# A two-block fp32 transformer kernel: dilated attention's steps moved inside the product tiles, the experts' first bias in fp32r, another order of the first loads, the recurrence spread over slots

## The reference, cut to what matters

```
ada = silu(c) @ w_ada + b_ada                       # 6 vectors: shifts, scales, gates
h = rmsnorm(x) * (1 + sc1) + sh1;  proj = h @ w_in + b_in
xr = conv4(xr);  r, i = sigmoid(xr @ w_a), sigmoid(xr @ w_x)   # block diagonal
a = exp(-8 r softplus(-lam));  state[t] = a state[t-1] + sqrt(1 - a*a) (xr i)[t]
y_att = softmax(q k - slope*dist, with a sink) v     # band of 128, 16 heads
x += g1 * rmsnorm(merge(state, y_att) @ w_out)
# experts: logits -> top 4 of 32 -> for each expert
act = swiglu(x_e @ w1[e] + b1[e]);  y += gate * (act @ w2[e] + b2[e])
# second block, layer 1:
qkv = hn @ w_qkv -> 3 groups (dilation 1, 4, 16) x (q, k, v) x 16 heads x 64
q, k = rmsnorm per head;  logits = q k + bias[g, head, distance]
o = softmax over the keys of all three groups together, times v;  h += o @ w_out
```

## Time and profile before

| | us |
|---|---|
| median of 3 executions | 2758.9 (2754.11 to 2763.45) |
| profiled execution, its own time | 2752.79 |
| profiled execution, span | 2751.0 |
| PE busy in the span | 2546.6 (93%) |
| DVE busy | 1377.2 (50%) |
| ACT busy | 1040.5 (38%) |
| matmul clock granted, mean | 0.94 of full |
| memory read | 670 MB, 244 GB/s mean |

### The profile page before, as it was taken

How to read it: one execution, slowest core, us unless ns; L and a number is a source line. 1 busy time by engine, 2 the same in 40 slices (tenths; PEclk the granted TensorE clock), 3 DMA queues, 4 the chain that set the end, 5 groups by cost and what they waited for, 6 DMA issues and landing times.

```text
span 2751.0 us, 36239 instructions
## 1 busy us (share of the span) xinstructions
PE 2546.6 (93%) x13568; PEld 1736.4 (63%) x13569; DVE 1377.2 (50%) x2617; ACT 1040.5 (38%) x1827; POOL 69.9 (3%) x122
## 2 busy tenths in 40 slices
PE   5798969999999999999989999999998999999999
PEld 3566844433343333433348887888886778788788
DVE  4467742111221122112248778776775665554785
ACT  3545531211111111211136555655554665322653
POOL 0000000000000000000000000000001000110000
PEclk8899978999999999999999999999999999656999
DMA  7654347999999999999946555555655445430553
GB/s 269 208 184 153 123 192 290 408 405 410 410 409 409 406 410 401 407 405 411 409 175 199 183 185 168 184 176 177 198 188 157 153 139 170 89 36 4 175 189 126
DMA packets 310572, 673.37 MB, mean 245 GB/s; under 512 B 8421, under 2 KB 235920, under 8 KB 277537
## 3 DMA queue, kind: packets, MB, share of 16 engines
q1 hardware_dynamic: 307280, 663.40, 65.1%
q0 software_dynamic: 3184, 8.53, 2.3%
HBM read 670.25 MB, written 1.12 MB: 244 GB/s over the span
## 4 chain that ended last, share of the span: by engine, by line
PE 78%; DVE 11%; ACT 5%; issue 5%; DMA 1%; POOL 0%; DVEq 0%; ACTq 0%; POOLq 0%
PE PS L349 21%; PE PS L1240 16%; PE PS L350 11%; PE PS L1257 8%; PE PS L1226 4%; PE PS L357 3%; DVE WS L312 3%; PE PS L1749 3%; ACT WS L308 2%; PE PS L1232 2%; PE PS L1770 2%; PE PS L358 2%; PE PS L1757 1%; DVE LIN L1354 1%; DVE AC L1357 1%
## 5 line engine op out<-in xcount | busy, mean ns | idle before, releaser
L349 PE MATMUL PS<-HN,WS 128*128 128x512 f32 x1952 | 702.0, 403 | 20.2 <-DVE WS L312 15.3
L312 DVE TENSOR_TENSOR WS<-RAW,WS 128x1024 fp32r<-128x1024 f32 (+1 forms) x452 | 542.3, 1204 | 224.7 <-ACT WS L308 221.0
L350 PE MATMUL PS<-HN,WS 128*128 128x256 f32 x1952 | 549.5, 282 | 0.0
L308 ACT ACTIVATE WS<-RAW 128x1024 fp32r<-128x1024 f32 (+1 forms) x452 | 465.7, 1035 | 158.5 <-PE PS L358 88.7
L1240 PE MATMUL PS<-W,XG 128*64 128x512 f32 x2048 | 450.4, 598 | 0.0
L349 PEld LDWEIGHTS PS<-HN,WS 128*128 128x128 f32 x1952 | 370.7, 190 | 114.4 <-DVE WS L312 19.0
L1350 DVE TENSOR_SCALAR GLU<-PS 128x512 f32<-128x512 f32 x32 | 22.1, 692 | 729.0 <-PE PS L1240 729.0
L350 PEld LDWEIGHTS PS<-HN,WS 128*128 128x128 f32 x1952 | 373.3, 191 | 0.4
L1240 PEld LDWEIGHTS PS<-W,XG 128*64 128x64 f32 x2048 | 145.0, 138 | 303.9 <-issue 303.9
L1257 PE MATMUL PS<-W,AT 128*64 128x512 f32 x1024 | 226.8, 595 | 22.0 <-ACT AT L1158 22.0
L349 PE MATMUL PS<-MI,WS 128*128 128x512 f32 x704 | 245.4, 394 | 0.0
(11 more groups left out here) (339 smaller groups left out, 2772.2 us busy)
## 6 DMA issues: line engine op xcount, KB each, us to landing
W<-in_moe_w SPq DMA_DIRECT2D x192, 2048.0 KB, 10.7
RAW<-in_ffn_w_in SPq DMA_DIRECT2D x88, 1024.0 KB, 5.2
RAW<-in_attn_w_qkv SPq DMA_DIRECT2D x36, 1024.0 KB, 5.1
RAW<-in_ffn_w_out SPq DMA_DIRECT2D x32, 1024.0 KB, 5.0
RAW<-in_w_ada SPq DMA_DIRECT2D x24, 1024.0 KB, 8.5
RAW<-in_w_in SPq DMA_DIRECT2D x22, 1024.0 KB, 5.2
RAW<-in_ffn_w_out SPq DMA_DIRECT2D x16, 768.0 KB, 4.3
RAW<-in_conv_w_in SPq DMA_DIRECT2D x12, 1024.0 KB, 5.2
```

The source lines that it names most:

```text
L308: act_f(split_tile(0, n), raw_tile(n), ACT.Copy).then_inc(hi_done, 1)
L312: vec.tensor_tensor(split_tile(1, n), raw_tile(n), split_tile(0, n).bitcast(f32), ALU.subtract).then_inc(lo_done, 1)
L349: nc.tensor.matmul(both, hi[:, k, :], x2[:, :, kx, :], start=start, stop=False)
L350: ins = nc.tensor.matmul(half, lo[:, k, :], x2[:, 0, kx, :], start=False, stop=stop)
```

## The change

Six edits. (1) `attention_mixer` is rebuilt: `qk` and `v` become one layer `qkv` of four blocks of 18 tiles. A block holds one turn of four heads: six value tiles, then twelve query and key tiles; QK and VV hold two blocks. The ten steps of turn c stand inside tiles 4 to 10 of block c + 1, one before every sixth chunk, and its outputs are transposed and split behind tiles 11 and 13 there. Steps have one score place, one transpose place and one output place in PSUM; the stage copies (L1847, L1848) and the table ORD with its wait are gone; ACT alone copies the transposed weights. The last turn stands around the first three tiles of `attn_out`. (2) Layers can have three banks; where the number changes between layers, the first tiles wait for all evacuations. (3) In `tok` layers both tiles of a pair are split behind the odd tile. (4) Six `w_ada` pieces are loaded before the first two weight pairs, and the gate weights are loaded before the bias rows are stored. (5) `decay`, the root, the products and the scans are spread over s = 11 to 22. (6) The experts' bias is a high and a low part in fp32r over 128 rows, one matmul per bank; EH becomes 128 x 128.

```diff
+        order = [("ada", j) for j in range(ADA_FIRST - 2)] + [("unit", 0), ("unit", 2)]
+        order += [("ada", j) for j in range(ADA_FIRST - 2, ADA_FIRST)]
+        for n in range(4, len(unit), 2):
...
-            if u.n + SLOTS_W < stop:
+            if not L.tok and u.n + SLOTS_W < stop:
+                make(eng, u.n + SLOTS_W)
+            elif L.tok and u.n % 2:
+                make(eng, u.n + SLOTS_W - 1)
                 make(eng, u.n + SLOTS_W)
...
-                if u.first and L.t0 + u.tile >= 4:
-                    pe.wait_ge(evacuated, L.t0 + u.tile - 3)
+                if u.first and u.tile < L.banks and L.fresh_banks:
+                    pe.wait_ge(evacuated, L.t0)
+                elif u.first and L.t0 + u.tile >= L.banks:
+                    pe.wait_ge(evacuated, L.t0 + u.tile - L.banks + 1)
...
+            pool.wait_ge(sem("ada_mm"), ADA_FIRST - 1)
+            pool.dma_start(BDA[:, :, :], A["bd_a"]).then_inc(sem("bd_loaded"), 16)
+            pool.dma_start(BDX[:, :, :], A["bd_x"]).then_inc(sem("bd_loaded"), 16)
             pool.wait_ge(sem("rows_ready"), N_GROUPS)
...
-                if s in (11, 12):
-                    for c in range(4 * (s - 11), 4 * (s - 10)):
+                if 11 <= s < 15:
+                    for c in range(2 * (s - 11), 2 * (s - 10)):
                         decay(c)
...
+                if s == 15:
                     act.wait_ge(sem("half_tanh"), DC)
                     act_f(T1[:, :, :], T1[:, :, :], ACT.Sqrt).then_inc(sem("rnn_act"), 1)
...
-                if s == 14:
+                if s == 17:
                     dve.wait_ge(sem("rnn_act"), 1)
                     o.link(STT(T1[:, :, :], T3, 1.0, T1[:, :, :], ALU.add, ALU.mult))
...
+                if s == 18:
+                    o.wait()
                     TTN(T2[:, :, :], T2[:, :, :], T1[:, :, :], ALU.mult).then_inc(sem("lru_in"), 1)
-                if s in (15, 16):
+                if 19 <= s < 23:
...
-        sp.dma_start(B1[0:NE, :], A["moe_b1"][0]).then_inc(sem("b1_loaded"), 16)
+        for r in range(4):
+            sp.dma_start(B1[r * NE:(r + 1) * NE, :], A["moe_b1"][0][:, r // 2 * FF:(r // 2 + 1) * FF]).then_inc(sem("b1_loaded"), 16)
...
+            act.wait_ge(sem("b1_loaded"), 64)
+            act_f(B1S[:, :], B1[:, :], ACT.Copy).then_inc(sem("b1_split"), 1)
...
                     for j in range(2):
-                        for g in range(2):
-                            nc.tensor.matmul(bank[j][64 * g:64 * g + 64, :], EH[0:NE, :],
-                                             B1[0:NE, 1024 * g + 512 * j:1024 * g + 512 * (j + 1)], start=True, stop=False)
+                        nc.tensor.matmul(bank[j][:, :], EH[:, :], B1S[:, 512 * j:512 * (j + 1)], start=True, stop=False)
...
+            for half in range(2):
+                h = slice(half * SLOTS, (half + 1) * SLOTS)
+                o.mark(vec.memset(HALVES[h, h], 1.0))
+            for r in range(4):
+                h = slice(r * NE, (r + 1) * NE)
+                o.mark(vec.tensor_copy(PICK[h, :], IDENT[h, h]))
+            dve.wait_ge(sem("b1_split"), 1)
+            for r in (1, 3):
+                low = slice(r * NE, (r + 1) * NE)
+                TTN(B1S[low, :], B1[low, :], B1S[low, :].bitcast(f32), ALU.subtract).then_inc(sem("b1_split"), 1)
...
-                vec.tensor_copy(EH[0:NE, :], IDENT[0:NE, ds(e, 1)].to_broadcast([NE, SLOTS])).then_inc(sem("e_taken"), 1)
+                TS(EH[:, :], HALVES[:, :], PICK[:, ds(e, 1)], None, ALU.mult).then_inc(sem("e_taken"), 1)
...
+        STEP_BEFORE = {(4 + 6 * i // DC, 6 * i % DC): i for i in range(NU + 2)}
+        STEPS_AT = {w: [i for (v, k), i in STEP_BEFORE.items() if v == w + 1] for w in range(3, 10)}
+        LAST_BEFORE = {(1, 0): 0, (1, 3): 1, (2, 0): 2, (2, 3): 3}
+        OUT_AT = {11: 0, 13: 1}
...
             def scores(c, u):
+                pe.wait_ge(sem("q_taken"), 12 * (c + 1))
+                if U:
+                    pe.wait_ge(sem("b_biased"), U)
...
             def turn_keys(c, u):
+                pe.wait_ge(sem("b_exp"), U + 1)
+                if U:
+                    pe.wait_ge(sem("b_ET"), U)
...
             def weigh(c, u):
+                pe.wait_ge(sem("b_ET"), U + 1)
+                pe.wait_ge(evacuated, qkv.t0 + c * TURN_TILES + TURN_V)
+                if U:
+                    pe.wait_ge(sem("b_out"), U)
...
+            def step(c, i):
+                if i < NU:
+                    scores(c, i)
+                if 1 <= i <= NU:
+                    turn_keys(c, i - 1)
+                if i >= 2:
+                    weigh(c, i - 2)
...
+            def last_turn(t):
+                if t == 2:
+                    for i in range(len(LAST_BEFORE), NU + 2):
+                        step(TURNS - 1, i)
+                    for m in (DC - 2, DC - 1):
+                        turn_out(m)
+
+            products(pe, qkv, HN, feed=norm.wait_chunk, after=behind, defer=OPENING, inside=inside)
+            products(pe, ao, OXB, feed=lambda pe, k: pe.wait_ge(sem("ox_lo"), k + 1), defer=(3, DC - 2), between=last_turn,
+                     inside=last_inside)
```

More of the change, by code:

```diff
@@ L327, in run_layer, with dense_bank, products @@
                 behind(u.tile)
-    def products(pe, L, x2, feed=None, after=None, defer=(0, 0)):
+    def dense_bank(L, t):
+        return bank[(L.t0 + t) % 4] if L.banks == 4 else bank[t % L.banks]
+    def products(pe, L, x2, feed=None, after=None, defer=(0, 0), between=None, inside=None):
         fed = set()
@@ L363, in products @@
             for k in range(cut):
+                if inside is not None:
+                    inside(u.tile, k)
                 chunk_of(u, k)
+            if between is not None:
+                between(u.tile)
         for k in range(cut, DC):
@@ new lines, in out_high, with before, behind @@
+            def out_high(m):
+                act.wait_ge(sem("x_T"), m + 1)
+                act_f(OXH[:, m, :], bank[7][:, 0:S], ACT.Copy).then_inc(sem("ox_hi"), 1)
+            def before(s):
+                n = query(s - 1)
+                if n is not None:
+                    square(n, s - 1)
+                n = query(s - 2)
+                if n is not None:
+                    root(n)
+            def behind(s):
+                n = query(s - 3)
+                if n is not None:
+                    take(n)
+                c, w = s // TURN_TILES - 1, s % TURN_TILES
+                if 0 <= c < TURNS - 1:
+                    for i in STEPS_AT.get(w, ()):
+                        step(c, i)
+                    if w in OUT_AT:
+                        out_high(2 * c + OUT_AT[w])
@@ L1685, in work_qk, with work @@
+            def work(t):
                 if t == 0:
@@ L1716, in act, with transposes @@
+                before(t)
+            act.wait_ge(sem("gains_ready"), 6)
+            run_layer(act, qkv, hi_tile, work, behind)
+            for s in range(qkv.T, qkv.T + 3):
+                before(s)
+                behind(s)
+            for i in range(NU + 2):
+                step(TURNS - 1, i)
+            for m in (DC - 2, DC - 1):
+                out_high(m)
             update.act(act)
         def pe(pe):
-            def transposes(t):
-                pe.wait_ge(sem("q_normed"), t + 1)
-                if t >= 2:
-                    pe.wait_ge(sem("q_taken"), t - 1)
+            def transposes(n):
+                pe.wait_ge(sem("q_normed"), n + 1)
+                if n >= 2:
+                    pe.wait_ge(sem("q_taken"), n - 1)
+                if n >= 12:
+                    pe.wait_ge(sem("b_biased"), n // 12 * NU)
@@ new lines, in behind, with inside @@
+            def behind(s):
+                if s == 0:
+                    norm.pe_mean(pe, columns=True)
+                n = query(s - 3)
+                if n is not None:
+                    transposes(n)
+                c, w = s // TURN_TILES - 1, s % TURN_TILES
+                if 0 <= c < TURNS - 1 and w in OUT_AT:
+                    turn_out(2 * c + OUT_AT[w])
+            def inside(t, k):
+                c, at = t // TURN_TILES - 1, (t % TURN_TILES, k)
+                if 0 <= c < TURNS - 1 and at in STEP_BEFORE:
+                    step(c, STEP_BEFORE[at])
@@ L1830, in work_qk, with behind, work @@
+            def behind(s):
+                c, w = s // TURN_TILES - 1, s % TURN_TILES
+                if 0 <= c < TURNS - 1:
+                    for i in STEPS_AT.get(w, ()):
+                        step(c, i)
+                    if w in OUT_AT:
+                        out_low(2 * c + OUT_AT[w])
+            def work(t):
                 if t == 0:
@@ L1901, in dve @@
+                before(t)
+            run_layer(dve, qkv, lo_tile, work, behind)
+            for s in range(qkv.T, qkv.T + 3):
+                before(s)
+            for i in range(NU + 2):
+                step(TURNS - 1, i)
+            for m in (DC - 2, DC - 1):
+                out_low(m)
             update.dve(dve)
```

(3 more changed lines are left out.)

379 lines of the change are left out of this document (168 added, 211 removed).

## The result

The changed kernel takes 2634.97 us (median of 4 runs, 2630.53 to 2636.59), the kernel before 2759.94 (4 runs): ratio 0.9546, 95% interval 0.9528 to 0.9564. Forecast was 2650, range 2614 to 2700. The profiled execution of after has a span of 2634.4 us against 2751.0, so 116.6 us went. The new mean granted clock is 0.968 where it was 0.941.

A forecast was written before the change was run, and what follows sets the result against it. PE bounds nearly everywhere, at half clock in the attention loop, with transfers close beside it in the experts. 5.8 + 13.8 + 10 + 22 + 62 - 4.8 = 108.8 off 2752.8 gives 2644; median offset 6.1: 2650, range 2614 to 2700.

The forecast's parts named there:

- Start, gate weights: Kernel start to mixer tile 14: reordered loads end the transfers' pause, -5.8 us; earlier gate weights remove PE's wait, -13.8 us.
- Recurrence: Mixer tiles from 14 on: spreading decays, root, products and scans over more slots saves 10 us, bounds 4 and 18.
- Experts: Expert loop: cheaper bias, limited by transfers at 30.6 us an expert, plus 14 us of lead: -22 us net, bounds 14 and 43.
- PE waiting for a w1 or w2 landing: Expected sign in the expert loop: PE waits for weight landings, with a period of 30.4 to 30.7 us.
- my own sign of error: Expert loop: the prediction called itself wrong if the period per expert is under 30 us.
- Attention, blocks: The `qkv` blocks: 330 us from first chunk to last, with 31 us of waits and 3.39 us a query tile.
- my sign of error of 0.9: The `qkv` blocks: the prediction called itself wrong if the granted clock there is below 0.9.
- clock rival: Attention steps pull the clock down: to the layer's end, 2830 us, 5%; only in the 21 tiles with steps, 2748, 4%.
- Last turn: Attention's last turn: 51 us, six uncovered steps at the old loop's clock, 5.2 us each; wrong if over 65 us.
- Opening of the next stage: Stage behind attention: PE must wait for all evacuations, so its first tile comes later; 4.8 us charged.
- The rival that ACT and DVE bind: Attention blocks: every step waits for its full chain, 75 us of waits instead of 31, giving 2694 us; 16%.
- The rival that the transfers have room: Expert loop: PE's own 1.4 us per expert count in full, 43 us instead of 22, giving 2629 us; 10%.

The follow-up runs named there:

- experiment 1: The changed kernel with the old order of first loads and the gate weights loaded behind the bias rows again: 2651.6 us, 16.7 more than the changed kernel.
- experiments 5 and 6: Changed kernel with half of each expert's gather, first alone, then also half of w2 for every expert but the first: expert stage 981.9 and 949.2 us.
- experiment 3: The changed kernel with the experts' first bias in fp32 as before, without the set-up of the split bias: 2662.1 us, 27.1 more.
- experiment 8: The changed kernel without projection chunks between the last turn's steps: 63.5 us instead of 50.5 from last query tile to the projection's first evacuation.
- Experiment 10: Also written banks: the changed kernel with the output projection's tiles 3 to 7 in banks the last turn has left: 2626.0 us, ratio 0.9526 to before.
- experiment 5: The changed kernel with each expert's gather for the first 128 tokens alone, loads unchanged: expert stage 981.9 us instead of 986.2.

## Why the prediction was right, step by step

The forecast of 2650 was 15 us too long, 0.6%. About half of that is in the terms: the profiled executions differ by 116.2 us, the terms add up to 108.8. The other half is the 6.1 us that I added because before's median stood above its profiled execution; after's stands 1.6 us below it. By its own steps:

- **Start, gate weights.** 6.3 and 13.5 for 5.8 and 13.8, and the pause of the transfers is gone, as forecast. Undoing both costs 20.1 us at tile 14 (experiment 1).
- **Recurrence.** 7.7 for 10. I counted the new slots' overload but not that the scans, two a slot for four slots, make those tiles slower as well (6.1 us).
- **Experts.** This is the term that was mis-sized: 32.4 for 22. The mechanism, transfers that can't follow and a store that PE eats, was right (experiments 5 and 6). Two sizes were off and worked against each other. The floor is 30.16 us an expert, not 30.6, as I had taken w2's 392 GB/s from a short stretch (and 30.80 less 30.6 is a pause of 0.2 us, not the 0.3 that I summed); and PE saved 1.03, not 1.4, as the bias had been the cover of ACT's copy of XG, which I hadn't looked for. So PE ate 0.4 us an expert, 12 of the 14 us, and never met a landing. "PE waiting for a w1 or w2 landing" was wrong, and so was the period of 30.4 to 30.7: under 30 was my own sign of error. The set-up cost 5.8 for 4, the first expert (gather to w2, 414.75 to 445.7 against 391.59 to 418.75) gained 3.8 for 2.8, and 2.5 us lie behind. Of these, 1.7 are the one slow expert of before (experiment 3) and no part of the mechanism that I forecast; the last 0.8 us I can't place.
- **Attention, blocks.** From first to last chunk 325 us for 330, near by luck in its parts. Waits were 16 for 31. A query tile without steps took 3.24 us for 3.39, some 6 us in all: in the 7.27 us that I had read for two tiles, the wait of 0.51 had cost 0.8 with what stood around it. Against that stand 10 us for six stretches at 0.50 that I had put at nothing, a wait of 2.99 us for the first value tile, and 2 us in steps and outputs. The steps ran mostly at 1.00 in the tiles, as forecast, and the blocks' mean of 0.96 is above my sign of error of 0.9; neither clock rival came true.
- **Last turn.** 50.5 us for 51, by luck in its parts: the last queries took 9.5 for 7.5, the ten steps 34.5 for 39, what follows them 6.5 for 4.5. I forecast the loop's clock for the uncovered six and they had 1.00 for most of the way; experiment 8 shows what that is worth, and on what it hangs.
- **Opening of the next stage.** 6.3 lost for 4.8. Experiment 10 takes exactly that back.

The rival that ACT and DVE bind (2694) was half true at the end of a turn, where the table loads are, and nowhere else. The rival that the transfers have room (2629) gave the nearer number for another reason: they haven't, the store was large enough.

## What to carry to other kernels

Where PE and the transfers are close, look at how the time from issue to landing moves over the loop, not at who waits: a loop can run below the transfers' floor to its end on what has been loaded ahead, and the next saving in it is then worth nearly nothing. Work that is cut from PE uncovers what ran beside it (here a copy of 0.6 us, and a quarter of the gain went), so ask of each piece what waits behind it. Short dependent steps want dense work between them, for cover and, as far as one run without it shows, for the sake of the clock. A function that needs another table should stand clear of the last step: putting the steps half a tile earlier was worth 16.5 us here in the medians; of the 17.0 in the profiles, waits are 8.3 and the clock 6.8.

## What the runs showed of the hardware

- One program's dense stretch takes one of two times, 185.56 or 189.00 us, by 6.5 ns a chunk (two matmuls), at a granted clock of 1.00 in both; within one execution some stretches have the one and some the other. A difference of 3.4 us in one such stage of one profile says nothing of an edit.
- The last turn's steps ran mostly at 1.00 with three chunks of product ahead of each of the first four, and at 0.50 without (one execution), with PE busy for 5.00 of 5 us in most of those stretches and one wait of 0.74 us between the steps' start and the fall. In one profile with cover (banks) the clock was 0.50 for the first 15 us of steps all the same.
- A PE that is full by the profile isn't enough for the full clock: 0.72 from 1074 to 1080 us of before with 6.00 of 6 us busy.
- Across the 13 profiles with the new attention `qkv` takes 305.5 to 324.4 us, from first to last chunk. Waits of 10.9 to 19.3 us and half of the time at 0.50, which is 3 to 24 us, account for all of that but 2.5 us.
- Loads of 2 MB with the queue never empty move 417 GB/s, 30.16 us for 12.58 MB, in experiment 5 and in the changed kernel alike.
